# Eleven row slots and nine weight slots in place of fifteen and six, and five modulation buffers in place of seven

## The reference, cut to what matters

```
a = jnp.einsum('tkd,td->tk', u_tab[ei], hx)
w = gt * jax.nn.gelu(a, approximate=False)
return jnp.einsum('tk,tkd->td', w, v_tab[ei])
```

## Time and profile before

| what | value |
|---|---|
| median of 3 runs | 2528.47 us (2528.45 to 2529.8) |
| the profiled execution, its own time | 2524.74 us |
| its span | 2522.6 us |
| bytes moved | 969.16 MB, mean 384 GB/s |
| busy: PE, DVE, POOL, ACT | 1287.4, 1374.3, 1479.2, 283.7 us |
| row gathers | 1536, 937 ns of POOL each (median) |

### The profile page before, as it was taken

The page is one execution under the profiler, slowest core; times in us unless marked ns, Lnnn a source line. Parts: engine busy times, 40 slices in busy tenths (PEclk is TensorE's granted clock), DMA queues, the critical chain, the costliest instruction groups (busy, mean ns, idle before and its releaser), DMA issues.

```text
span 2522.6 us, 21875 instructions
## 1 busy us (share of the span) xinstructions
PE 1287.4 (51%) x7582; PEld 714.4 (28%) x7582; DVE 1374.3 (54%) x3238; ACT 283.7 (11%) x616; POOL 1479.2 (59%) x1583
## 2 busy tenths in 40 slices
PE   3888774596420155545565467589530023333554
PEld 1647663453100143223331047366100000000111
DVE  0224998936389955545433368845469974444000
ACT  0221332210000011100000023221000000000000
POOL 0010464656677655465667665445777677777774
PEclk7889885898655577677887678699655555555778
DMA  9798898999999999999999999799999999999998
GB/s 356 272 385 306 299 409 321 399 409 409 383 409 409 381 365 409 390 387 395 409 409 409 406 409 409 296 384 346 393 409 410 385 410 409 409 409 410 407 409 335
DMA packets 269349, 969.16 MB, mean 384 GB/s; under 512 B 38420, under 2 KB 40468, under 8 KB 262840
## 3 DMA queue, kind: packets, MB, share of 16 engines
q0 software_dynamic: 227232, 849.45, 85.4%
q1 hardware_dynamic: 39664, 117.22, 12.4%
q10 hardware_dynamic: 2344, 1.09, 0.2%
HBM read 962.38 MB, written 5.27 MB: 384 GB/s over the span
## 4 chain that ended last, share of the span: by engine, by line
DMA 32%; DVE 25%; PE 20%; POOL 13%; issue 6%; ACT 2%; ACTq 1%; SPq 0%; POOLq 0%; DVEq 0%
DVE ring L754 17%; DMA ring<-in_v,eV 15%; DMA ring<-in_u,eU 14%; POOL ring L414 9%; PE ps L1200 7%; PE ps L1409 4%; POOL ring L409 3%; PE ps L1243 3%; DMA wada<-in_wada 2%; PE ps L1381 1%; ACTq L439 1%; PE ps L1102 1%; PE ps L1217 1%; PE ps L1247 1%; DVE pick L1059 1%
## 5 line engine op out<-in xcount | busy, mean ns | idle before, releaser
L754 DVE CUSTOM_DVE_ANT_0 ring<-ring,ps 128x1024 f32<-128x1024 f32 x768 | 904.6, 1218 | 485.1 <-DMA ring<-in_u,eU 359.6
L409 POOL DMA_INDIRECT ring<-in_u,eU x768 | 728.3, 948 | 504.8 <-DVE adot L754 166.2
L414 POOL DMA_INDIRECT ring<-in_v,eV x768 | 727.8, 948 | 345.4 <-issue 170.3
L1200 PE MATMUL ps<-ring,Wd 128*32 128x512 f32 x3072 | 556.1, 861 | 647.7 <-DMA ring<-in_v,eV 644.5
L1200 PEld LDWEIGHTS ps<-ring,Wd 128*32 128x32 f32 x3072 | 114.7, 137 | 1012.2 <-issue 1007.5
L1409 PE MATMUL ps<-h,wring 128*128 128x128 f32 (+1 forms) x1024 | 191.5, 342 | 21.7 <-ACT h L513 15.3
L1409 PEld LDWEIGHTS ps<-h,wring 128*128 128x128 f32 x1024 | 162.2, 200 | 77.5 <-issue 57.2
L1243 PE MATMUL ps<-h,wring 128*128 128x128 f32 (+1 forms) x768 | 142.4, 348 | 35.9 <-ACT h L513 20.8
L1243 PEld LDWEIGHTS ps<-h,wring 128*128 128x128 f32 x768 | 126.8, 208 | 58.3 <-issue 45.5
L955 DVE MAX8 sv<-sc 128x8 f32<-128x128 f32 x160 | 40.7, 287 | 183.3 <-ACT sc L421 181.5
L1176 PE MATMUL ps<-cst,eF 128*128 128x128 f32 x6 | 2.5, 417 | 234.1 <-DVE eU L1065 234.1
(11 more groups left out here) (203 smaller groups left out, 1093.8 us busy)
## 6 DMA issues: line engine op xcount, KB each, us to landing
wada<-in_wada POOLq DMA_DIRECT2D x42, 1024.0 KB, 14.0
wring<-in_win SPq DMA_DIRECT2D x72, 512.0 KB, 7.0
wring<-in_wpq SPq DMA_DIRECT2D x64, 576.0 KB, 7.3
wring<-in_wout SPq DMA_DIRECT2D x32, 512.0 KB, 7.3
ring<-in_u,eU POOLq DMA_INDIRECT x768, 8.2
ring<-in_v,eV POOLq DMA_INDIRECT x768, 9.2
wada<-in_wada SPq DMA_DIRECT2D x6, 1024.0 KB, 13.2
wring<-in_ckT SPq DMA_DIRECT2D x8, 512.0 KB, 8.0
```

Of the source, the lines that this page charges most:

```text
L409: g.indirect_dma_start(ring[p % NR][:], None, a["u"], bass.IndirectOffsetOnAxis(ap=eU[t % 3][:, i:i + 1], axis=0)).then_inc(ld_r[p % NR], 16)
L414: g.indirect_dma_start(ring[p % NR][:], None, a["v"], bass.IndirectOffsetOnAxis(ap=eV[t % 3][:, tok:tok + 1], axis=0)).then_inc(ld_r[p % N ...
L754: nc.vector.tensor_tensor_reduce(ring[p % NR][:], ring[p % NR][:], ps[:, 0:2, :].rearrange("p b d -> p (b d)"), 1.0, 0.0, ALU.mult, ALU.ad ...
L1200: ins = mm(ps[QUAD * q:QUAD * q + QUAD, 2 + half, :], Wd[:, QUAD * q + c, :], ring[at4[q] % NR][:, half * 512:(half + 1) * 512], start=(c ...
```

## The change

The row ring shrinks from 15 slots to 11 (60 KB to 44 KB of each partition), the weight ring grows from six to nine (27 KB to 40.5 KB). As the modulation buffers lie inside the row ring, they go from seven to five, and SP loads four of the chunks at the start in place of six; POOL loads the other 44. `ORDER`, the ticks and all arithmetic stay.

```
-NWR = 6
+NWR = 9
...
-NR = 15
+NR = 11
...
-ADA_SP = 6
-ADA_BUF = 7
+ADA_SP = 4
+ADA_BUF = 5
...
-wada = [... (WD, WD + 8192, G0 + 28672, G0 + 36864, G0 + 45056, G0 + 53248, G0 + 10240)[s]) ...]
+wada = [... (WD, WD + 8192, G0 + 28672, G0 + 36864, G0 + 10240)[s]) ...]
...
-            load_ada(4)
-            load_ada(5)
```

More of the change, by code:

```diff
@@ L243, in build @@
         sifs = scratch("sif", [2 * PH, TOPK], W + 33280, WD + 11776, BF16)
-        wada = [at(f"wada{s}", [ADA_W], (WD, WD + 8192, G0 + 28672, G0 + 36864, G0 + 45056, G0 + 53248, G0 + 10240)[s]) for s in range(ADA_BUF)]
+        wada = [at(f"wada{s}", [ADA_W], (WD, WD + 8192, G0 + 28672, G0 + 36864, G0 + 10240)[s]) for s in range(ADA_BUF)]
         brev = [at(f"brev{k}", [H, keys[k]], G0 + (0, 4096, 6144)[k]) for k in range(3)]
```

## The result

The changed kernel takes 2831.43 us (median of 4 runs, 2826.38 to 2840.91) against 2528.46 of the kernel before: a ratio of 1.1207, 95% interval 1.1177 to 1.1237. The forecast was 2671 us, 2608 to 2722. The direction was right and the mechanism stands in the trace where the prediction put it, but the price was more than double: 303 us in place of 143. The profiled execution takes 2828.0 us, its span is 2826.2.

What follows compares the result with a forecast made beforehand. The prediction took the DMA engines, mostly at 409 GB/s, to bound the kernel. Mixed batches 94, unit 2's front 40, other stretches 8 and weights and buffers 1 sum to 143 us: about 2671 us, range 2608 to 2722.

Steps and rivals of the forecast that it cites:

- The cycle of a mixed batch: Mixed stretches without a front: batches take 12.3 us instead of 10.24; 46 batches cost 94 us, bounds 85 and 108.
- L = 4.5: Landing time assumed for the next mixed batch's last v row, from three successive rows landing after 4.5 to 4.8 us.
- the lone row's 4.3: Shortest landing of a gathered row finding the queues nearly empty; as low bound it gives a 12.09 us mixed cycle.
- about 3: Mixed stretch with 15 slots: of the 7.4 us landing, about 3 us are queue time, all the slack there.
- The stretch with unit 2's front: Mixed rows beside unit 2's front, 28 batches: weights fill part of the new gaps; cost 40 us, bounds 0 and 57.
- Stretches of u or v alone: Unmixed stretches keep the full rate and lose only when stalls end: 8 us, bounds 0 and 20.
- at 1.3 us each: Cost assumed per stall around 420 us and at five or six other dips, with 5.1 us behind the last.
- The weight ring and the modulation buffers: Nine weight slots and five modulation buffers, mainly unit 0's front: + 1 us net, from - 6.3 to + 6.
- so this wait goes: PE's 6.3 us wait for unit 0's first `pq` chunk was to vanish with nine weight slots.
- The rule for a GpSimd DMA: Cited in the shorter-landings rival (about 2612 us, chance 0.10): 3.2 us per row, 46 batches costing 35 us.
- Heavier: Rival: front bursts add in unit 2's stretch and each stall opens the whole 5.1 us; about 2749 us, chance 0.05.
- the running stretch's 7.4 us: Landing time of rows issued at POOL's stop in the mixed stretch with 15 slots, 7.4 to 7.8 us.

Runs made afterwards that it cites:

- the loads cut down: Unit 2's weight loads carry only 64 columns of a chunk: 2776.05 us on the whole change, 2483.89 us on the kernel before.
- blocks of four: Mixed order four u, four v rows instead of alternating: 2570.05 us on the whole change (11 slots), 2517.09 us on the kernel before (15).

## Why the prediction was wrong, point by point

**The cycle of a mixed batch: mechanism right, one term mis-sized.** The step that failed is "With L = 4.5 (the middle of the three isolated rows, which were issued 1.24 us apart as these are". The batch waits for the fourth row behind POOL's stop, and that took 6.2 us: 13.9 us a batch in place of 12.3, and 156 us in place of 94. The row stood in the trace before: the three rows are the first three behind a stop, and the next one, issued at 2004.65, is

```profile
L409 POOL DMA_INDIRECT ring<-in_u,eU x1: 934/934/934, 2004.6 to 2004.6; - x1
DMA to landing us min/median/max: 5.5/5.5/5.5
```

and the one behind that takes 6.0. The reading stopped one row short of the row in question. That row's 5.5 us would have given 13.3 us a batch, nearer, but still short of the 13.9. Taking the lone row's 4.3 as the low bound was right for the first row only. The slack read with these short landings, "about 3" us, was too much as well: by the forecast's own sum 13 slots would take 3.94 + 1.24 + 4.5 + 0.13 = 9.81 us and cost nothing, and they cost 0.8 us a batch.

**The stretch with unit 2's front.** "a value nearer the upper bound, 40 us" of an upper bound of 57 failed twice: the gap was mis-sized, as above, and none of it is filled. With the loads cut down, 11 slots cost 394.9 - 304.4 = 90.5 us here over 15; the weights do not lower that but add 14 us to it, to the 104 measured. The reason given, that a chunk travels beside the awaited rows, was right, and the landing times with and without the weights (8.1 and 6.2 us) show it; it should have led to the upper bound itself.

**Stretches of u or v alone.** Their steady cycles kept nearly the full rate, as forecast (v alone 403 GB/s at the end, where the kernel before has 406; u alone 409 to 410 from 2100 to 2150 us). Yet these stretches did not lose 8 us but 41, twice the upper bound of 20. The two kernels in blocks of four, 11 slots against 15, lose some 33 us there, mostly in the first 40 rows, the v rows behind unit 2's stretch, and unit 3's front. So the step that failed is the term "at 1.3 us each" for the stalls. Why each costs more stays open; that the refill after each stall pays the slow restart too is argued, not shown.

**The weight ring and the modulation buffers.** "so this wait goes" was wrong: the chunk is held by SP's own issue of the pool output and the prompt, and moving them is what removes most of the wait. The sum of + 1 us came near the 2.4 us in the profile, but that is no proof of its parts: the first gathers of kernels with the same unit 0 as the kernel before lie from 264.0 to 267.2 us.

**The rivals.** The rule for a GpSimd DMA of the Trainium skill, "DMA: Bandwidth & Descriptors", section "Anatomy of one DMA — SWDGE (gpsimd) path", gives an estimated 3.2 us for such a row. These runs do not agree with it, counted from the start of POOL's issue as the sum counts: 4.3 us for the first row behind a stop, 6.2 for the fourth. Counted from the end of the issue, 0.94 us later, the first row's 3.4 us is near it. "Heavier" (2749 us) came nearest. Its term for the stalls, 7 x 5.1 = 36 us, is near the 41 measured, but most of what the forecast missed came by another way than its mechanism: one landing time in 74 batches.

**The range.** Its upper end took L from 4.3 to 4.8, the spread of one group of three rows, as the bounds. A term that counts 74 times needed wider bounds: the running stretch's 7.4 us was the other near row, and the true value lies between.

## What to carry to other kernels

The depth that this ring needs is set by the longest hold of its oldest slot plus the landing time of the row that takes its place; work the chain for the very row that the consumer waits for, with a landing read for that row's place behind the stop, not for a lone transfer. Where several slots are released together, put their rows next to each other in the order: that shortened the hold from six rows to three, was worth 261 us with 11 slots and 11 us with 15, and took no memory. Weights that are released by the same engine that releases the rows arrived here together with the rows it needed next, and filled none of its gaps.

## What the runs showed of the hardware

- With 11 slots a 512 KB gather of POOL lands 4.3 us after the start of its issue when the engines have run dry; the second, third and fourth take 5.3, 5.8 and 6.2 us. With 14 slots, where the stream runs at 409 GB/s, none of that stretch with its landing in the trace takes less than 6.2. After 1 us of rest the engines moved 134 GB/s for 1.5 us though they were 71% busy.
- The ring's cost has a knee: 13, 63, 184 and 299 us for 14, 13, 12 and 11 slots.
- The issue of one DMA held SP's queue for 13 us (the prompt's load in the changed kernel, behind the pool outputs), and all loads behind it.
